# A sixth row buffer for the expert stage, gathers issued five at a time, Pool drains moved, and the last product on two engines

## The chip, the cores and the metric

The kernel runs on one core of one Trainium2 chip. Its engines are called here as the profile calls them: PE (TensorE, matmuls; PEld is its weight load), DVE (VectorE), ACT (ScalarE), Pool (GpSimd) and SP (SyncE, which only issues DMAs). The metric is the device time of one execution in microseconds (us). A row of a profile is stamped in us from the start of the execution.

## The reference, cut to what matters

The program is two transformer blocks over 512 tokens of width 1024, in float32. Of the second block only its end bears on the change: a mixture of 32 experts in 4 groups, two experts per token, and the last norm.

```python
h2 = rmsnorm_2(x, norm2_g[l])
x = x + hier_moe(h2, ...)      # per token: gate * (silu(h @ w_gate[e]) * (h @ w_up[e])) @ w_down[e], two e
return rmsnorm_2(x, norm_f_g)  # y * rsqrt(mean(y * y) + 1e-6) * g
```

An expert has three matrices of 1 MB each (1024x256, 1024x256 and 256x1024).

## The kernel before, in words

Everything ahead of the expert stage (about the first 1050 us) is dense layers and attention; the change leaves it as it is. By the end of it the 512 rows going into the experts lie in DRAM as `x_rows`, and `part_rows`, also 512 rows in DRAM, holds zeros.

The expert stage works in 17 **units** (`UNITS_E`, q = 0 to 16, `LAST_E` = 16). A unit is two halves of 64 rows, each for one expert, so it takes the weights of two experts, 6 MB (unit 8, `EXTRA_AT`, uses one expert for both halves). A small routing program on DVE writes the table `tabi`, a column per unit: which rows to gather (1), where to scatter (0), and for which tokens this is the second and last expert (2), whose rows are finished. Entries for nothing are out of bounds and skipped. What that program finds out late (more rows for an expert than fit, the experts of the later units) it signals as `over_listed` and `over_ready`; the latter comes from `name_late_experts` in unit 1.

Per unit the steps are these; the engines run apart and meet at semaphores:

- **Pool** gathers the rows of the unit from `x_rows` into a row buffer `xe` (L691, `gather`, up to four units ahead, `X_FIRST`), later gathers the partial results from `part_rows` into the same buffer (L699, `gather_parts`, "the parts"), scatters the unit's sum back (L695, `scatter`) and stores the finished rows to `out` (L703, `store_rows`). All are indirect DMAs of Pool's own queue, issued in program order. Parts of unit q+1 may only be gathered once the scatter of unit q has landed (`scattered`). For units 8 and 9 (`MIXED_E`) this stands behind the other steps of the unit before instead of ahead of them.
- **PE** transposes the gathered rows (L2066, `turn_rows_of`), multiplies with the gate and up weights (L2408, `gate_up_part`), transposes the hidden rows (L2066, `turn_hidden`) and multiplies with the down weights (L2425, `down`). For units 1 to 12 (`AHEAD_E`) the first quarter of the gates is done ahead, beside the unit before.
- **DVE** scales the transposed rows (L1759), makes the hidden product (L1766, `hidden`), adds the down result onto the parts (L1776, `y_of`) and, one unit later, multiplies the finished rows by their norm factor and by `gfin`, the final norm vector (L1787, `finish`). It works in program order, so `hidden` of unit q+1 stands behind `y_of(q)` and `finish(q-1)`.
- **ACT** makes the silu (L1159), copies (L1162), and sums squares for the norm (L1170, `squares_of`) in two halves of 512 columns; it ends in a guess of the inverse root that DVE refines.
- **SP** issues all weight loads, each as soon as the buffer is free: six gate/up buffers (`gu`, three units) and eight down buffers (`dn`, four units). For units 3 and 4 (`PIECED_E`) gates and ups are loaded by quarters as PE frees them (L613). SP also loads `gfin` (L602).

The last unit is done by halves of 512 columns: down, `y` (L2004), squares; then DVE's `finish` and Pool's last store. `pool.drain()` stands at q = 13 and 15 (L742), ahead of the wait for `y_made`.

Space sets where the row buffers lie. `xe` has six of 4 KB per partition. Buffers 4 and 5 lie over the scratch tables of the routing program, so before `over_listed` and `over_ready` only four can be filled. The order of use is:

```python
def buffer_of(q):
    return q if q < X_FIRST else (0, 1, 4, 5, 2, 3)[(q - X_FIRST) % X_BUFS]
```

`gfin` lies over the rotation tables (`cos`, `sin`), which are no longer needed by then.

## Time and profile before

| | |
|---|---|
| median of three runs | 1306.07 us (1304.95 to 1306.09) |
| the profiled execution: its own time | 1303.1 us |
| the profiled execution: span from first to last instruction | 1301.1 us |
| mean granted clock of PE | 0.992 of full speed (2.4 GHz) |
| busy share of PE / DVE / ACT / Pool | 96% / 49% / 40% / 44% |
| matmuls L2408 (gate and up), 1088 of them | 128.4 us, 386 ns each |
| matmuls L2425 (down), 256 of them | 61.4 us, 624 ns each |
| DMAs of gates, ups and downs: median time from issue to landing | 15.4, 16.3 and 17.8 us |
| DMA rate in the 34th to 39th of 40 slices | 386, 417, 416, 417, 417 and 417 GB/s, the slices before 331 and 359 |

How to read it: the shares of busy time are means over very different stages. The expert stage is the last fifth, and its limit is to be read from that stretch alone. The span and the profiled time are one execution, 3 us under the median of the runs. A wait in the profile is given as idle time of an engine ahead of an instruction, with what ended it. Pool's busy time counts the issue of a DMA (about 1 us each), not its transfer; "us to landing" is from issue until the last piece has arrived.

### The profile page before, as it was taken

How to read it: one execution, taken by the hardware profiler on the slowest of the kernel's cores; microseconds unless marked ns; L12 is line 12 of the kernel's file. 1: busy time of each engine (PE TensorE's matmuls, PEld its weight loads, DVE VectorE, ACT ScalarE, POOL GpSimd, SP SyncE). 2: the span in 40 equal slices, each digit the busy share in tenths (PEclk: the TensorE clock that was granted, in tenths of full speed). 3: DMA queues.
4: the chain of work that ended last, by engine and by line, in shares of the span. 5: the costliest groups of instructions: out<-in, count | busy, mean ns of one | idle time of the engine just before them, and what ended most of it. 6: DMA issues, size and time to landing. Idle time of an engine off the chain costs nothing.

```text
span 1301.1 us, 18979 instructions
## 1 busy us (share of the span) xinstructions
PE 1255.3 (96%) x6642; PEld 960.5 (74%) x6642; DVE 640.0 (49%) x1248; ACT 522.9 (40%) x884; POOL 568.9 (44%) x715
## 2 busy tenths in 40 slices
PE   7999999999999999999999999999999989998896
PEld 6767777787888888888888788777888865554462
DVE  4868768725542422222225765757243276342443
ACT  5657544435444324133144534145322300543444
POOL 4633323334655655555545664424644212341321
PEclk9999999999999999999999999999999999998899
DMA  6422222112334333333333333322427999999996
GB/s 219 109 65 55 67 58 65 50 49 81 98 96 113 115 97 97 115 97 113 97 98 97 97 96 83 82 49 70 126 81 265 359 331 386 417 417 416 417 417 246
DMA packets 223104, 208.38 MB, mean 160 GB/s; under 512 B 36034, under 2 KB 197556, under 8 KB 218804
## 3 DMA queue, kind: packets, MB, share of 16 engines
q1 hardware_dynamic: 209728, 191.87, 44.7%
q0 software_dynamic: 9504, 13.66, 2.8%
q10 hardware_dynamic: 3796, 1.86, 0.5%
q8 instruction: 45, 0.74, 0.2%
q14 instruction: 31, 0.25, 0.1%
HBM read 209.43 MB, written 20.45 MB: 177 GB/s over the span
## 4 chain that ended last, share of the span: by engine, by line
issue 40%; POOL 31%; PE 19%; DMA 4%; DVE 3%; SPq 2%; POOLq 1%; ACT 0%; DVEq 0%; ACTq 0%
POOL wlo L670 31%; PE bank L2408 4%; PE bank L2036 3%; PE bank L2038 3%; PE bank L2037 3%; PE bank L2425 3%; SPq L543 1%; DMA gu<-in_w_exp_up 1%; DMA xe<-part_rows,tabi 1%; PE side L2066 1%; DMA part_rows<-xe,tabi 1%; DMA xe<-x_rows,tabi 1%; PE side L2038 1%; PE side L2037 1%; PE side L2036 1%
## 5 line engine op out<-in xcount | busy, mean ns | idle before, releaser
L670 POOL TENSOR_TENSOR wlo<-raw,whi 128x256 fp32r<-128x256 f32 x644 | 497.6, 804 | 525.9 <-ACT whi L838 525.7
L2037 PE MATMUL bank<-actB_lo,whi 128*128 128x512 f32 x608 | 236.7, 389 | 0.0
L838 ACT ACTIVATE whi<-raw 128x1024 fp32r<-128x1024 f32 x161 | 169.0, 1051 | 152.6 <-PE bank L2038 125.0
L2036 PE MATMUL bank<-actB_hi,whi 128*128 128x512 f32 x576 | 227.8, 395 | 0.5 <-POOL wlo L670 0.5
L2038 PE MATMUL bank<-actB_hi,wlo 128*128 128x512 f32 x576 | 224.4, 390 | 0.0
L2036 PE MATMUL bank<-actA_hi,whi 128*128 128x512 f32 x400 | 157.0, 392 | 1.7 <-DVE actA_lo L1269 1.6
L2038 PE MATMUL bank<-actA_hi,wlo 128*128 128x512 f32 x400 | 155.7, 389 | 0.0
L2037 PE MATMUL bank<-actA_lo,whi 128*128 128x512 f32 x400 | 155.7, 389 | 0.0
L2408 PE MATMUL bank<-gu,xeT 128*64 128x256 f32 x1088 | 128.4, 386 | 8.5 <-issue 5.9
L2037 PEld LDWEIGHTS bank<-actB_lo,whi 128*128 128x128 f32 x608 | 114.2, 188 | 24.0 <-issue 1.0
L2036 PEld LDWEIGHTS bank<-actB_hi,whi 128*128 128x128 f32 x576 | 108.2, 188 | 25.9 <-issue 2.3
L2038 PEld LDWEIGHTS bank<-actB_hi,wlo 128*128 128x128 f32 x576 | 108.1, 188 | 22.8
L2408 PEld LDWEIGHTS bank<-gu,xeT 128*64 128x64 f32 x1088 | 80.6, 139 | 51.5 <-issue 19.3
L2059 PE MATMUL bank<-actA_hi,whi 128*128 128x512 f32 x216 | 95.0, 440 | 0.0
L2036 PEld LDWEIGHTS bank<-actA_hi,whi 128*128 128x128 f32 x400 | 75.1, 188 | 19.5 <-DVE actA_lo L1269 3.5
L2038 PEld LDWEIGHTS bank<-actA_hi,wlo 128*128 128x128 f32 x400 | 75.1, 188 | 15.8
L2037 PEld LDWEIGHTS bank<-actA_lo,whi 128*128 128x128 f32 x400 | 75.1, 188 | 15.3 <-issue 0.2
L1464 DVE TENSOR_SCALAR relu_u<-bank 128x512 f32<-128x512 f32 x32 | 22.1, 692 | 128.7 <-PE bank L2038 128.7
L2061 PE MATMUL bank<-actA_hi,wlo 128*128 128x512 f32 x216 | 85.0, 393 | 0.0
L2060 PE MATMUL bank<-actA_lo,whi 128*128 128x512 f32 x216 | 84.5, 391 | 0.0
L1478 DVE TENSOR_TENSOR ytmp<-bank,rs 128x512 f32<-128x512 f32 x32 | 22.1, 692 | 95.8 <-PE bank L2038 95.8
L2425 PE MATMUL bank<-dn,hidT 128*64 128x512 f32 x256 | 61.4, 624 | 2.7 <-ACT hidT L1162 2.7
(448 smaller groups left out, 1703.3 us busy)
## 6 DMA issues: line engine op xcount, KB each, us to landing
gu<-in_w_exp_gate SPq DMA_DIRECT2D x64, 512.0 KB, 15.4
gu<-in_w_exp_up SPq DMA_DIRECT2D x64, 512.0 KB, 16.3
dn<-in_w_exp_down SPq DMA_DIRECT2D x30, 1024.0 KB, 17.8
raw<-in_w_in SPq DMA_DIRECT2D x57, 512.0 KB, 3.8
raw<-in_w_up SPq DMA_DIRECT2D x32, 512.0 KB, 3.9
raw<-in_w_down SPq DMA_DIRECT2D x32, 512.0 KB, 3.7
raw<-in_w_out SPq DMA_DIRECT2D x16, 512.0 KB, 3.8
raw<-in_w_in SPq DMA_DIRECT2D x16, 256.0 KB, 3.2
```

Source lines behind the costliest of these rows:

```text
L670: ins = nc.gpsimd.tensor_tensor(wlo[:, slot, at], raw[:, slot, at], whi[:, slot, at].bitcast(F32), ALU.subtract)
L838: a(whi[:, c % RING, :], raw[:, c % RING, :], ACT.Copy).then_inc(hi_made, 1)
L1464: chain(v.tensor_scalar(relu_u[:, m % 2, :], out_bank(up + m)[:, :], 0.0, None, ALU.max), chunk_freed)
L1478: chain(v.tensor_tensor(ytmp[:, :], out_bank(c)[:, :], rs[:, :], ALU.mult), chunk_freed)
L2036: mm(b[:, :], w_hi, hi[:, k, :], start=first, stop=False)
L2037: mm(b[:, :], w_hi, lo[:, k, :], start=False, stop=False)
L2038: ins = mm(b[:, :], w_lo, hi[:, k, :], start=False, stop=last)
L2059: mm(b[:, :], w_hi, actA_hi[:, k, :], start=k == 0, stop=False)
L2060: mm(b[:, :], w_hi, actA_lo[:, k, :], start=False, stop=False)
L2061: ins = mm(b[:, :], w_lo, actA_hi[:, k, :], start=False, stop=k == NK - 1)
L2408: ins = mm(b[ROWS * h:ROWS * (h + 1), g * DE:(g + 1) * DE], xeT[:, j, k, ROWS * h:ROWS * (h + 1)], gu[n % GU_BUFS][:, g, k, :], start=k == ...
L2425: ins = mm(bank[2 + n][ROWS * h:ROWS * (h + 1), :], hidT[:, j, k * P + ROWS * h:k * P + ROWS * (h + 1)], w[:, k, n * L:(n + 1) * L], start ...
```

## The change

- **A row buffer elsewhere.** `xe` shrinks to five buffers, and the sixth, `xe_far`, lies where `gfin` was, over the rotation tables. It is free from the start. `buffer_of` becomes (5, 4, 0, 1, 2, 3) from unit 4 on, so unit 4 uses the new buffer and unit 5 the one over the scratch tables.
- **Gathers.** Five gathers are issued at once instead of four. The gather of unit 5 waits for `over_listed` alone and no longer for the scatter of unit 1; the waits for scatters 0 and 1 and for `over_ready` go.
- **The norm vector in two pieces.** `gfin0` lies over another table (`before`) and is loaded where `gfin` was; `gfin1` lies behind the five buffers, over routing scratch, so SP waits for `over_ready` first, after the quarters of unit 4. DVE waits for both pieces in unit 3. Each product by the norm is two instructions of 512 columns instead of one of 1024.
- **Drains.** The drain at q = 13 goes, that at q = 15 stays; at q = 7 and 8 a drain is put in behind the store, ahead of `scattered(q)` and the parts of units 8 and 9.
- **The last unit.** `finish_last`: DVE multiplies both halves by the norm vector once each half's squares are taken (`last_squared`), then refines the norm (`last_norm_made`), then DVE scales the first half and ACT the second; Pool's last store waits for both.
- The path for overflowing rows gets the same pieces and other semaphore counts; it isn't run with these inputs.

The diff, cut to its core (the lines of `x_in` in place of `xe[:, n, :]` are shown once):

```diff
@@ -42,7 +42,7 @@
 
 def buffer_of(q):
 
-    return q if q < X_FIRST else (0, 1, 4, 5, 2, 3)[(q - X_FIRST) % X_BUFS]
+    return q if q < X_FIRST else (5, 4, 0, 1, 2, 3)[(q - X_FIRST) % X_BUFS]
 
 
 OVER_X = buffer_of(LAST_E + 1)
...
@@ -362,13 +362,13 @@
         dn_at = (*(s_at + n * half_buf for n in range(7)), b_at + 3 * half_buf)
         gu = [place(f"gu{n}", [P, 2, NK, DE], gu_at[n]) for n in range(GU_BUFS)]
         dn = [place(f"dn{n}", [P, 2, D], dn_at[n]) for n in range(D_BUFS)]
-        xe, _ = lay(b_at, ("xe", [P, X_BUFS, D]))
+        xe, gfin_at = lay(b_at, ("xe", [P, X_BUFS - 1, D]))
         hid, row_at, after4, after8, end3 = lay(s_at + 7 * half_buf, ("hid", [P, 2, DE]), ("row_at", [P, 2 * NT]),
                                  ("after4", [P, NG, NG]), ("after8", [P, EPG, EPG]))
...
@@ -377,9 +377,14 @@
         steps64, tabi, over_n, over_at, spare_rows, tab_end = lay(low_at + words([P, 2, NK, P]) + words([P, 2, DE]),
                                        ("steps64", [P, 8]), ("tabi", [P, 3, COLS], I32), ("over_n", [1, 2 * OVER + 1], I32),
                                        ("over_at", [P, 3], I32), ("spare_rows", [P, 1], I32))
-        below = place("below", [1, OVER, NE], b_at + words([P, X_FIRST + 1, D]))
+        below = place("below", [1, OVER, NE], gfin_at)
         slotv = place("slotv", [P, 2, COLS], -(-tab_end // 64) * 64)
-        gfin = place("gfin", [P, D], base + 4 * CONST_COLS["cos"][0])
+        xe_far = place("xe_far", [P, D], base + 4 * CONST_COLS["cos"][0])
+        gfin = (place("gfin0", [P, L], base + 4 * CONST_COLS["before"][0]), place("gfin1", [P, L], gfin_at))
+
+        def x_in(n):
+            return xe[:, n, :] if n < X_BUFS - 1 else xe_far[:, :]
+
         lg, gw, vals, pos, pos_q, over_v, _ = lay(
             base + 4 * CONST_COLS["cos_tok"][0], ("lg", [P, NT, NG + NE]), ("gw", [P, 16, NT]),
             ("vals", [P, 2 * NT, 3]), ("pos", [P, 2 * NT]), ("pos_q", [P, 2 * NT]), ("over_v", [P, 4]))
...
                 sp.wait_ge(S(f"x_stored{n}"), 16 * NK // 2)
-            sp.dma_start(gfin[:, :], A["norm_f_g_2"].partition_broadcast(P)).then_inc(S("small_in"), 16)
+            sp.dma_start(gfin[0][:, :], A["norm_f_g_2"][0:L].partition_broadcast(P)).then_inc(S("small_in"), 16)
             def gate_up_in_quarters(q):
...
@@ -621,6 +626,9 @@
                         down(n)
                 if q in PIECED_E:
                     gate_up_in_quarters(q)
+                    if q == PIECED_E.stop - 1:
+                        sp.wait_ge(S("over_ready"), 1)
+                        sp.dma_start(gfin[1][:, :], A["norm_f_g_2"][L:].partition_broadcast(P)).then_inc(S("small_in"), 16)
                     continue
                 for n in places_of(q):
                     sp.wait_ge(S("gate_up_done"), unit_of(n - GU_BUFS) + 1)
...
             def gather(n, rows, done):
-                pool.indirect_dma_start(xe[:, n, :], None, x_rows, bass.IndirectOffsetOnAxis(ap=rows, axis=0),
+                pool.indirect_dma_start(x_in(n), None, x_rows, bass.IndirectOffsetOnAxis(ap=rows, axis=0),
                                         bounds_check=row_bound, oob_is_err=False).then_inc(done, 16)
 
...
 
-            for q in range(X_FIRST):
-                gather(q, tabi[:, 1, q:q + 1], S(f"gathered{q}"))
+            for q in range(X_FIRST + 1):
+                gather(buffer_of(q), tabi[:, 1, q:q + 1], S(f"gathered{q}"))
...
@@ -738,23 +746,21 @@
                     scattered(q - 1)
                 if FINISH_FROM <= q + 1 < LAST_E and q + 1 not in MIXED_E:
                     parts_of_unit(q + 1)
-                if q in (LAST_E - 3, LAST_E - 1):
+                if q == LAST_E - 1:
                     pool.drain()
                 pool.wait_ge(S("y_made"), q + 1)
                 scatter(buffer_of(q), tabi[:, 0, q:q + 1], S(f"scattered{q % 2}"))
                 n = q + X_FIRST
-                if n < UNITS_E:
-                    if q < 2:
-                        scattered(q)
-                    if q == 2:
+                if X_FIRST < n < UNITS_E:
+                    if q == 1:
                         pool.wait_ge(S("over_listed"), 1)
-                        pool.wait_ge(S("over_ready"), 1)
                     if q - 2 >= FINISH_FROM:
                         pool.wait_ge(S("rows_stored"), 16 * (q - 1 - FINISH_FROM))
                     gather(buffer_of(n), tabi[:, 1, n:n + 1], S(f"gathered{n % X_BUFS}"))
                 if q > FINISH_FROM:
                     store_unit(q - 1)
                 if q + 1 in MIXED_E:
+                    pool.drain()
                     scattered(q)
                     parts_of_unit(q + 1)
             over = over_count(pool)
...
@@ -788,6 +794,7 @@
             scattered(LAST_E - 1)
             for n in range(X_BUFS):
                 pool.wait_ge(S(f"gathered{n}"), 16 * ((LAST_E - n) // X_BUFS + 1))
+            pool.wait_ge(S("last_squared"), 3)
             store_unit(LAST_E)
 
 
...
@@ -1167,7 +1174,8 @@
                 nc.scalar.preload_act_table_set("natural_log_exp_and_others")
                 for n in range(2):
                     act.wait_ge(*((S("y_made"), q + 1) if q < LAST_E else (S("last_y_made"), n + 1)))
-                    chain(a(side[3][:, :], xe[:, buffer_of(q), n * L:(n + 1) * L], ACT.Square, accum_out=gw[:, 10 + n, one_]))
+                    chain(a(side[3][:, :], x_in(buffer_of(q))[:, n * L:(n + 1) * L], ACT.Square, accum_out=gw[:, 10 + n, one_]),
+                          S("last_squared") if q == LAST_E else None)
                     if n == 0:
                         chain(a(gw[:, 3, one_], gw[:, 10, one_], ACT.Identity, scale=1.0 / D, bias=eps_t[:, :]))
                 chain(a(gw[:, 14, one_], gw[:, 11, one_], ACT.Ln, scale=1.0 / D, bias=gw[:, 3, one_]))
...
@@ -1784,8 +1795,22 @@
                 refine(gw[:, 12, one_], gw[:, 13, one_], D, gw[:, 14, one_], gw[:, 15, one_])
                 if q < LAST_E:
                     dve.wait_ge(S(f"scattered{q % 2}"), 16 * (q // 2 + 1))
-                chain(v.scalar_tensor_tensor(xe[:, buffer_of(q), :], xe[:, buffer_of(q), :], gw[:, 13, one_], gfin[:, :],
-                                             ALU.mult, ALU.mult), S("rows_finished"))
+                for n in range(2):
+                    x = x_in(buffer_of(q))[:, n * L:(n + 1) * L]
+                    ins = v.scalar_tensor_tensor(x, x, gw[:, 13, one_], gfin[n][:, :], ALU.mult, ALU.mult)
+                chain(ins, S("rows_finished"))
+
+            def finish_last():
+
+                one_ = slice(LAST_E % NT, LAST_E % NT + 1)
+                first, second = (x_in(buffer_of(LAST_E))[:, n * L:(n + 1) * L] for n in range(2))
+                for n, x in enumerate((first, second)):
+                    dve.wait_ge(S("last_squared"), n + 1)
+                    chain(v.tensor_tensor(x, x, gfin[n][:, :], ALU.mult))
+                dve.wait_ge(S("guess_made"), guesses[0] + 1)
+                chain(v.tensor_tensor(gw[:, 12, one_], gw[:, 10, one_], gw[:, 11, one_], ALU.add))
+                refine(gw[:, 12, one_], gw[:, 13, one_], D, gw[:, 14, one_], gw[:, 15, one_], made=S("last_norm_made"))
+                chain(v.tensor_scalar(first, first, gw[:, 13, one_], None, ALU.mult), S("rows_finished"))
 
             every_expert = const("iota")[:, 0:NE]
             cnt, extra, upto, before = (prod[:, 0, NE * n:NE * (n + 1)] for n in range(4))
...
                     rows_turned(q % 2, q + 3)
                 y_of(q)
-                if q == FINISH_FROM:
-                    dve.wait_ge(S("small_in"), 16 * (N_SMALL + 1))
+                if q == FINISH_FROM + 1:
+                    dve.wait_ge(S("small_in"), 16 * (N_SMALL + 2))
...
             dve.wait_ge(S(f"parts_in{LAST_E % 2}"), 16 * ((LAST_E - FINISH_FROM) // 2 + 1))
             for n in range(2):
-                x = xe[:, buffer_of(LAST_E), n * L:(n + 1) * L]
+                x = x_in(buffer_of(LAST_E))[:, n * L:(n + 1) * L]
                 dve.wait_ge(S("last_down_done"), n + 1)
                 v.scalar_tensor_tensor(x, bank[2 + n][:, :], slotv[:, 1, LAST_E:LAST_E + 1], x,
                                        ALU.mult, ALU.add).then_inc(S("last_y_made"), 1)
-            finish(LAST_E)
+            finish_last()
 
```

How the instructions stand on the engines. **Pool, start of the expert stage**, before (`xe<-x_rows` is a gather of rows, `xe<-part_rows` one of parts, `part_rows<-xe` a scatter):

```order
L691 DMA xe<-x_rows,tabi 128x1024 [waits rows_ready,x_stored1,x_stored0]
L691 DMA xe<-x_rows,tabi 128x1024 x3
L695 DMA part_rows<-xe,tabi 512x1024 [waits y_made,y_zeroed,slots_ready]
L691 DMA xe<-x_rows,tabi 128x1024 [waits scattered0]
L699 DMA xe<-part_rows,tabi 128x1024 [waits xe_used,scattered0]
L695 DMA part_rows<-xe,tabi 512x1024 [waits y_made]
L691 DMA xe<-x_rows,tabi 128x1024 [waits scattered1]
L699 DMA xe<-part_rows,tabi 128x1024 [waits xe_used,scattered1]
L695 DMA part_rows<-xe,tabi 512x1024 [waits y_made]
L691 DMA xe<-x_rows,tabi 128x1024 [waits over_ready,over_listed]
```

and now (`xe_far` is the new buffer):

```order
L699 DMA xe<-x_rows,tabi 128x1024 [waits rows_ready,x_stored1,x_stored0]
L699 DMA xe<-x_rows,tabi 128x1024 x3
L699 DMA xe_far<-x_rows,tabi 128x1024
L703 DMA part_rows<-xe,tabi 512x1024 [waits y_made,y_zeroed,slots_ready]
L707 DMA xe<-part_rows,tabi 128x1024 [waits xe_used,scattered0]
L703 DMA part_rows<-xe,tabi 512x1024 [waits y_made]
L699 DMA xe<-x_rows,tabi 128x1024 [waits over_listed]
L707 DMA xe<-part_rows,tabi 128x1024 [waits xe_used,scattered1]
L703 DMA part_rows<-xe,tabi 512x1024 [waits y_made]
L699 DMA xe<-x_rows,tabi 128x1024
```

The fifth gather stands with the first four, the one behind the first scatter is gone, and the next gather stands behind the second scatter with a wait for `over_listed` where it waited for `scattered1`. Drains are not listed in these rows; the diff shows their place.

**SP, end of the quarters of unit 4** (`gu_140`, `gu_141`) and the down weights of unit 5 (`dn_146`, `dn_147`), before:

```order
L613 DMA gu_140<-in_w_exp_up 128x1024 [waits gate_up_done]
L613 DMA gu_141<-in_w_exp_up 128x1024
L548 DMA dn_146<-in_w_exp_down 128x2048 [waits down_done]
L548 DMA dn_147<-in_w_exp_down 128x2048 [waits down_done]
L543 DMA gu_142<-in_w_exp_gate 128x1024 [waits gate_up_done]
```

and now:

```order
L618 DMA gu_140<-in_w_exp_up 128x1024 [waits gate_up_done]
L618 DMA gu_141<-in_w_exp_up 128x1024
L631 DMA gfin_176<-in_norm_f_g 128x512 [waits over_ready]
L553 DMA dn_146<-in_w_exp_down 128x2048 [waits down_done]
L553 DMA dn_147<-in_w_exp_down 128x2048 [waits down_done]
L548 DMA gu_142<-in_w_exp_gate 128x1024 [waits gate_up_done]
```

The second piece of the norm vector, with its wait, stands ahead of the down weights and all that follows.

**DVE, the end of the program**, from the second half of the last y, before (`gw` are the norm's small values):

```order
L2004 SCALAR_TENSOR_TENSOR xe<-bank,slotv,xe 128x512 [waits last_down_done]
L1783 TENSOR_TENSOR gw<-gw 128x1 [waits guess_made]
L1232 TENSOR_SCALAR gw<-gw 128x1 [waits guess_made,dve_step]
L1233 TENSOR_TENSOR gw<-gw 128x1 [waits dve_step]
L1234 TENSOR_TENSOR gw<-gw 128x1 [waits dve_step]
L1235 SCALAR_TENSOR_TENSOR gw<-gw 128x1 [waits dve_step]
L1787 SCALAR_TENSOR_TENSOR xe<-xe,gw,gfin 128x1024 [waits dve_step]
```

and now:

```order
L2031 SCALAR_TENSOR_TENSOR xe_far<-bank,slotv,xe_far 128x512 [waits last_down_done]
L1809 TENSOR_TENSOR xe_far<-xe_far,gfin_175 128x512 [waits last_squared]
L1809 TENSOR_TENSOR xe_far<-xe_far,gfin_176 128x512 [waits last_squared,dve_step]
L1811 TENSOR_TENSOR gw<-gw 128x1 [waits guess_made,dve_step]
L1243 TENSOR_SCALAR gw<-gw 128x1 [waits guess_made,dve_step]
L1244 TENSOR_TENSOR gw<-gw 128x1 [waits dve_step]
L1245 TENSOR_TENSOR gw<-gw 128x1 [waits dve_step]
L1246 SCALAR_TENSOR_TENSOR gw<-gw 128x1 [waits dve_step]
L1813 TENSOR_SCALAR xe_far<-xe_far,gw 128x512 [waits last_norm_made]
```

The 1024 wide product at the end became two products by the vector ahead of the norm's five small steps and one scaling of 512 columns behind them.

## Rows read from the trace of the kernel before

**Rows 1.** windows, 1096 to 1283 us (columns in its first line)

```profile
core 0: us, PE busy (x) PEld busy (x) DVE busy (x) ACT busy (x) POOL busy (x), PEclk, DMA share, GB/s
...
1096.00:1283.00 187.00, 169.07 (x1204) 95.34 (x1202) 68.17 (x145) 80.58 (x151) 58.39 (x54) 0.95 1.03 416
```

**Rows 2.** chain of waits at the end: start us, us, what

```profile
1264.90 18.86 DMA gu<-in_w_exp_up
...
1295.98 1.29 DVE xe L1787
```

**Rows 3.** timeline of PE: start us, us, what [idle before <-releaser]

```profile
1093.68 1.15 PE L2066 MATMUL side<-con,xe 128*128 128x128 f32 x8 [0.89 <-DMA xe<-x_rows,tabi]
...
1107.39 1.15 PE L2066 MATMUL side<-con,xe 128*128 128x128 f32 x8 [1.55 <-DMA xe<-x_rows,tabi]
...
1144.73 1.08 PE L2408 MATMUL bank<-gu,xeT 128*64 128x256 f32 x8
...
1206.52 0.69 PE L2066 MATMUL side<-con,hid 128*128 128x128 f32 x2 [4.11 <-DVE hid L1766]
...
1273.11 0.44 PE L2066 MATMUL side<-con,hid 128*128 128x128 f32 x2 [1.56 <-DVE hid L1766]
...
1283.80 3.67 PE L2408 MATMUL bank<-gu,xeT 128*64 128x256 f32 x32 [0.81 <-DMA gu<-in_w_exp_up]
```

**Rows 4.** timeline of DVE, the last instruction ahead of over_ready

```profile
1093.50 0.14 DVE L1908 CAST over_n<-prod 1x1 int32<-1x1 f32 x1
```

**Rows 5.** DMA issues near 1073, 1087 and 1125 us, last column us to landing

```profile
dn<-in_w_exp_down SPq DMA_DIRECT2D x2, 1024.0 KB, 6.2
...
dn<-in_w_exp_down SPq DMA_DIRECT2D x2, 1024.0 KB, 11.1
...
gu<-in_w_exp_gate SPq DMA_DIRECT2D x1, 512.0 KB, 19.1
```

**Rows 6.** Pool drains: ns min/median/max, first and last start us

```profile
L742 POOLq DRAIN  x2: 1967/6010/10054, 1247.0 to 1274.4; - x2
...
L257 POOLq DRAIN  x1: 3053/3053/3053, 1297.9 to 1297.9; - x1
```

**Rows 7.** timeline of Pool, the DMAs around the drains

```profile
1167.62 1.03 POOL L703 DMA_INDIRECT out<-xe,tabi  x1 [0.31 <-issue]
1177.13 1.02 POOL L699 DMA_INDIRECT xe<-part_rows,tabi  x1 [8.48 <-DMA part_rows<-xe,tabi]
...
1189.86 1.02 POOL L703 DMA_INDIRECT out<-xe,tabi  x1 [0.31 <-issue]
1194.30 1.02 POOL L699 DMA_INDIRECT xe<-part_rows,tabi  x1 [3.43 <-DMA part_rows<-xe,tabi]
...
1247.20 1.02 POOL L699 DMA_INDIRECT xe<-part_rows,tabi  x1 [3.28 <-DMA part_rows<-xe,tabi]
1257.78 1.02 POOL L695 DMA_INDIRECT part_rows<-xe,tabi  x1 [9.55 <-issue]
...
1298.07 0.98 POOL L703 DMA_INDIRECT out<-xe,tabi  x1 [6.49 <-DVE xe L1787]
```

**Rows 8.** DMA issues near 1167, 1189, 1247 and 1298 us: us to landing

```profile
out<-xe,tabi POOLq DMA_INDIRECT x1, 12.4
...
out<-xe,tabi POOLq DMA_INDIRECT x1, 10.2
...
xe<-part_rows,tabi POOLq DMA_INDIRECT x1, 7.5
...
out<-xe,tabi POOLq DMA_INDIRECT x1, 2.6
```

**Rows 9.** waits, 1045 to 1302 us: us in total, times, longest

```profile
DVE xe L1776 <- DMA xe<-part_rows,tabi: 25.3, 2, 14.4
```

**Rows 10.** instructions on tile xe: duration ns min/median/max

```profile
L1776 DVE SCALAR_TENSOR_TENSOR xe<-bank,slotv,xe x32: 740/748/753, 1075.1 to 1280.2; 128x512 f32<-128x512 f32 x32
L1170 ACT ACTIVATE side<-xe x30: 601/601/603, 1111.7 to 1293.7; 128x512 f32<-128x512 f32 x30
```

69 lines of the change are left out of this document (37 added, 32 removed).

## The prediction, as put on record

> **What bounds the kernel now.** I read four views: the busy time by stretches, the chain of waits at the end, the timelines of PE, SP, DVE and Pool over the expert stage, and the DMA issues of single moments with their time to landing. Up to about 1050 us the change moves nothing, so only the expert stage counts. From 1096 to 1283 us the 16 DMA engines are full: 416 GB/s at a share of 1.03, while PE works 169 of 187 us [rows 1]. So the expert weights arrive at a fixed pace, and their stream ends when its bytes are through. The chain ends accordingly: the last quarter of up weights, issued at 1264.90, lands 18.86 us later, and then come the last matmuls and the norm [rows 2]. But PE is nearly as late. It waits for those weights a mere 0.81 us, and from 1207 us on no other wait of it is longer than the 1.56 us at 1273.11 [rows 3]. Two limits lie on each other: the end moves with whichever gets later, and an early PE gains nothing. What can be delayed without harm is 0.81 us on PE and nothing on the stream.
>
> **Part 1: the second piece of the final norm vector (SP).** SP now waits for over_ready behind the quarters of unit 4, ahead of the down weights of unit 5. DVE's last instruction ahead of that signal ends at 1093.64 [rows 4]; SP issued those down weights at 1087.66, as the DMA issues of that moment show [rows 5]. So it stands some 6 us, and all of the stream's later issues are queued behind it. What hides part of this is the queue: the last quarters land near 1093 us. A pair of down weights issued into a nearly empty queue, at 1073.0, took 6.2 us in the median; the pair of 1087.66 took 11.1 behind the backlog and landed about 1087.85 + 11.1 = 1098.95 [rows 5]. New: the norm piece goes out at 1093.7, the pair at about 1094.2, and lands at 1094.2 + 6.2 + 0.6 (256 KB at 416 GB/s) = 1101.0. The stream shifts by **+2.1 us**. Bounds: 0 (the queue still had bytes, and the traffic of Pool fills the hole) and +3.5 (all of the time between 1093.0 and the first bytes of an issue at 1094, plus the piece itself).
>
> **Part 2: five gathers at once (Pool).** Row buffer 5 now lies where the rotation tables were, so unit 4 needs no buffer freed by unit 0, and unit 5 goes after scatter 1 is issued, not after it has landed. The two stalls of PE for gathered rows, 0.89 and 1.55 us [rows 3], go: PE is 2.44 us earlier from unit 4 on. What is late next are the gate weights of unit 7: issued at 1125.0, landed 19.1 us later at 1144.1 [rows 5], and PE used them at 1144.73 [rows 3], 0.6 us after. With the stream 2.1 us late, PE stands there until 1146.2. So ahead of unit 8 PE is 2.1 - 0.6 = **1.5 us later** than before, and the 2.44 us are spent. The fifth gather itself, about a microsecond of Pool, falls into an idle stretch: 0.
>
> **Part 3: the drains (Pool).** This is the large term. The trace records three drains. They end at 1247.0 + 10.05 = 1257.0, at 1274.4 + 1.97 = 1276.4 and at 1297.9 + 3.05 = 1300.9 [rows 6]. The parts issued at 1247.20 landed 7.5 us later, at 1254.7, and the scatter behind the first drain went out only at 1257.78, 9.55 us idle [rows 7, 8]. An empty drain would have taken nothing. I read a drain on Pool as a wait for every DMA it has in flight. The one removed (unit 13) delayed a scatter that nobody waited for, since PE's longest wait after 1207 us is that 1.56 us for `hidden` of unit 15; worth 0. The one kept (unit 15) stays. The two new ones stand at units 7 and 8, behind the gather and the store and ahead of the wait for the scatter. The program waited there for the scatter alone; now it waits for the store issued 2.65 us behind it as well.
> Unit 7: the store issued at 1167.62 took 12.4 us and landed at 1180.0; the parts of unit 8 went out at 1177.13 [rows 7, 8]. New: 1180.0 + 1.5 (part 2) + 0.25 (the nearer of the two ends to a landing seen, the last drain) + 0.3 (issue) = 1182.1, that is +4.9. Their landing released y of unit 8 after DVE had stood idle for them, the longer (14.4 us) of its two waits for parts, 25.3 us together [rows 9]: fully on the path. So scatter, gather and store of unit 8 are 4.9 later too.
> Unit 8: the store issued at 1189.86 took 10.2 us: 1200.1 + 4.9 = 1205.0, with 0.55 again 1205.5; the parts of unit 9 went out at 1194.30 [rows 7, 8]: **+11.2**. DVE stood idle for them too, the other 10.9 us [rows 9], and behind y of unit 9 on DVE stand the product of unit 8 and `hidden` of unit 10, for which PE waited 4.11 us at 1206.52 [rows 3]. Nothing cushions that; PE is 11.2 us late from there to the end. That unit's down weights can't help, since PE's wait is for DVE.
> What each drain ends behind its last landing is between 0.25 us (last drain: the store of 1298.07 took 2.6, so 1300.7, and the drain ended at 1300.9 [rows 6 to 8]) and 2.3 us (first: 1254.7, ended 1257.0); I take 0.25, as there a store was last in flight, as here. The other end adds 2 x 2.05 = 4.1 us.
>
> The Trainium skill (DMA: Bandwidth & Descriptors, Anatomy of one DMA) gives a Pool DMA about 2.0 us plus its bytes at 436 GB/s; by that estimate a store would land 2.65 us after the scatter ahead of it, each drain would cost 2.65 + 0.55 = 3.2, and the sum below would be +6.8 instead of +10.1. The rows here say 10.2 and 12.4 us for one store, so the trace does not agree, and the sum goes by the rows.
>
> **Part 4: products and the tail.** The product by the norm vector, once 1024 wide, is now two of 512. Nearest row: 0.75 us each [rows 10], 1.50 against the 1.29 of the chain [rows 2]; I take +0.15 as two of one line overlap (0.0 to 0.2), on the path once, ahead of `hidden` of unit 10. In the last unit DVE multiplies both halves by the vector while ScalarE finds the norm. The second half has to wait for the second square and ends about 0.2 us behind the guess; then after the refinement the two engines scale a half each, ScalarE in 0.60 us [rows 10], instead of 1.29 on DVE alone. Net: 0.2 + 0.05 + 0.6 - 1.29 = **-0.45 us**, between 0 and -0.8. The new `last_squared` wait of Pool stands with the wait it had.
>
> **Sum.** PE path: 11.2 + 0.15 - 0.81 (its slack) - 0.45 = **+10.1 us**. The stream's own end (+2.1 - 0.45) lies below that and is hidden. SP's issues for units 14 to 16 wait for a PE that is 11 us late, but the last loads took some 18.9 us to land because they queued [rows 2], where 6.2 is what an empty queue takes [rows 5]: the queue has nearly 13 us to give, and the stream ends before PE asks for it: 0. The profiled execution took 1303.1 us with a span of 1301.1; the median of the runs is 1306.07. The sum is put on the median: **1316.0 us**. What can be told from no change is 0.2%, or 2.6 us: 1303.5 to 1308.7.
>
> **The rivals.**
> (a) *A new drain costs nothing*: it ends when the scatter has landed, as the program waited there anyway. For it: the drain at 1274.4 took only 2 us, and none of the records shows what it looks at. Against it: the 9.55 us gap. Then the stream is the bound, +2.1 - 0.45 = +1.65: **1307.7**, 1305.5 to 1309.5 with the bounds of part 1.
> (b) *Faster*: the pace of the stream is set by SP's issues, and these by PE's releases, so the two vanished gather stalls come through. Place: gathers 4 and 5, from 1093 us on. Price: -2.44 - 0.45 = -2.9: **1303.2**. It decides if the queue doesn't run dry at over_ready and the drains are free as in (a). Against it: a DMA share of 1.03 for 187 us.
> (c) *Drains end late*, 2.3 us behind each landing like the first one: +14.2, **1320.3**; I count it with the forecast.
> (d) *The extra buffer is no help*: gather 5 lands after PE wants it, 1.55 us stay. PE stands for the gates of unit 7 anyway, so the end is that of the forecast; only the trace would tell.
>
> **How the numbers follow.** Forecast with (c): 0.75; its own range is from 8.0 (stream shift 0, so PE is 0.6 us early at unit 7 and not 1.5 late) to 10.1 + 4.1 + 1.4 = 15.6 us, 1314 to 1321.7. (a) 0.19, (b) 0.03, slower for another reason 0.03. The range reaches down into (a) at 1307.5 and up to 1321.5; that leaves out about 0.2. Faster: (b) and a sliver of (a), 0.04. Same: most of (a), 0.16. Slower: 0.80.
>
> **What would show it.** Right: drain records at units 7 and 8 of 10 us or more, the parts of unit 9 issued some 11 us later, a PE wait near 15 us ahead of the transposes of unit 10 where 4.11 stood, no PE wait for the last up weights, a DMA share under 1 after 1215 us. SP's pair of down weights near 1094 us with a hole in the stream before it; no PE wait for x_rows; a PE wait of some 4 us for the gates of unit 7. Wrong: short drains with parts of unit 9 within 3 us of their old place relative to PE, or a last PE wait for up weights still there.

## The result, and the profile after

| | before | after |
|---|---|---|
| median | 1305.51 us (1303.0 to 1306.09, 4 runs) | 1321.53 us (1319.77 to 1325.15, 4 runs) |
| ratio to before | 1 | 1.0130, 95% interval 1.0104 to 1.0156 |
| the profiled execution: time, span | 1303.1, 1301.1 us | 1319.77, 1317.7 us |
| mean granted clock of PE | 0.992 | 0.984 |

The changed kernel is slower by 16 us. I had forecast 10 (1316.0, from 1307.5 to 1321.5; 1306.07 + 10.1 is in fact 1316.2): the direction was right, the amount too small, and the result lies just above the range.

Where the time comes in is read from PE's starts at fixed places of the program:

| PE starts | before | after | later by | forecast |
|---|---|---|---|---|
| first gates of unit 0 | 1057.70 | 1058.66 | 0.96 | 0 |
| first gates of unit 7 | 1144.73 | 1149.10 | 4.37 | 1.5 |
| first gates of unit 9 | 1174.91 | 1180.61 | 5.70 | 1.5 |
| transposes of `hidden` of unit 10 | 1206.52 | 1221.59 | 15.07 | 11.2 |
| down products of the last unit | 1289.15 | 1305.86 | 16.71 | 10.5 |
| end of the span | 1301.1 | 1317.7 | 16.6 | 10.1 |

Between units 9 and 10 stand the two new drains: 9.4 us, where I had 9.7. All other stages gave more than I had. PE's timeline of the changed kernel, at the places of [rows 3]:

```profile
1058.66 7.13 PE L2435 MATMUL bank<-gu,xeT 128*64 128x256 f32 x64 [0.71 <-DVE xeT L1770]
...
1149.10 1.98 PE L2435 MATMUL bank<-gu,xeT 128*64 128x256 f32 x8 [5.02 <-DMA gu<-in_w_exp_gate]
...
1180.61 1.98 PE L2435 MATMUL bank<-gu,xeT 128*64 128x256 f32 x8 [3.11 <-issue]
...
1221.59 0.69 PE L2093 MATMUL side<-con,hid 128*128 128x128 f32 x2 [7.97 <-DVE hid L1777]
...
1249.34 0.44 PE L2093 MATMUL side<-con,hid 128*128 128x128 f32 x2 [1.33 <-DVE hid L1777]
1250.46 5.35 PE L2452 MATMUL bank<-dn,hidT 128*64 128x512 f32 x16 [0.68 <-ACT hidT L1169]
...
1297.09 7.11 PE L2435 MATMUL bank<-gu,xeT 128*64 128x256 f32 x64
```

The waits for gathered rows (0.89 and 1.55 us in [rows 3]) are gone, and so is the wait for the last up weights: the 64 matmuls at 1297.09 run in one piece. In their place stands 5.02 us for the gates of unit 7 and 7.97 for `hidden` of unit 10. The first eight gate matmuls behind the 5.02 us take 1.98 us, where they take 1.08 at full clock: the granted clock is at its lower level there (1.2 GHz; it is 0.50 from 1150 to 1152 us). Unit 12's down products take 5.35 instead of 3.65 for the same reason.

SP's side, with the stretches of the DMA engines (us, then busy time of each engine, PEclk, DMA share, GB/s), of the changed kernel:

```profile
1094.64 0.33 SPq L631 DMA_DIRECT2D gfin<-in_norm_f_g  x1
1095.01 1.05 SPq L553 DMA_DIRECT2D dn<-in_w_exp_down  x2
```

```profile
1088.00:1092.00 4.00, 4.00 (x38) 2.54 (x36) 3.23 (x7) 0.00 (x0) 1.38 (x2) 1.00 1.03 413
1092.00:1096.00 4.00, 4.00 (x36) 2.52 (x31) 3.58 (x15) 0.74 (x1) 1.41 (x2) 1.00 0.78 282
1096.00:1100.00 4.00, 4.00 (x24) 1.67 (x24) 0.45 (x1) 0.38 (x1) 0.42 (x1) 1.00 0.89 276
1100.00:1104.00 4.00, 4.00 (x38) 2.49 (x36) 1.68 (x4) 0.00 (x0) 1.28 (x2) 1.00 1.00 404
```

and the last three of these stretches of the kernel before:

```profile
1092.00:1096.00 4.00, 3.11 (x26) 1.91 (x22) 3.41 (x11) 0.70 (x1) 0.00 (x0) 1.00 1.04 428
1096.00:1100.00 4.00, 4.00 (x24) 1.66 (x24) 0.00 (x0) 0.38 (x1) 0.03 (x1) 1.00 0.99 411
1100.00:1104.00 4.00, 4.00 (x38) 2.50 (x36) 1.74 (x4) 0.00 (x0) 3.08 (x4) 1.00 1.03 420
```

The hole that the prediction spoke of is there, and it is larger: in twelve microseconds (428 - 282 + 411 - 276 + 420 - 404) x 4 = 1.2 MB less are moved, 2.9 us at 416 GB/s. What is moved holds the piece as well, 0.25 MB or 0.6 us, so by this count the weights fall back by 3.5 us.

The drains (ns min/median/max, first and last start), and Pool's DMAs around them, of the changed kernel:

```profile
L763 POOLq DRAIN  x2: 10698/11452/12207, 1175.0 to 1198.2; - x2
```

```profile
1173.47 1.01 POOL L703 DMA_INDIRECT part_rows<-xe,tabi  x1 [7.70 <-DVE xe L1787]
...
1187.98 1.02 POOL L707 DMA_INDIRECT xe<-part_rows,tabi  x1 [10.80 <-issue]
1196.66 1.01 POOL L703 DMA_INDIRECT part_rows<-xe,tabi  x1 [7.66 <-DVE xe L1787]
...
1209.66 1.02 POOL L707 DMA_INDIRECT xe<-part_rows,tabi  x1 [9.29 <-issue]
```

The records last 12.2 and 10.7 us. They begin ahead of the store's own issue (1175.0 and 1198.2, the stores at 1176.17 and 1199.35), so they are a little longer than what Pool stands for: 10.8 and 9.3 us idle ahead of the parts. The parts of unit 9 go out 13.0 us behind the scatter of unit 8; before it was 1194.30 [rows 7] less 1187.21, the scatter's issue there, or 7.1.

### The profile page after: what moved, and what is told of

It is laid out like the page before. It is cut to its first block, busy times and chain, and to the rows that moved or that the text cites. A ratio compares the mean times of both kernels' runs of the same rounds, so it can differ in the third digit from the quotient of the medians.

```text
span 1317.7 us, 19000 instructions
## 1 busy us (share of the span) xinstructions
PE 1264.5 (96%) x6642; PEld 967.5 (73%) x6642; DVE 637.2 (48%) x1264; ACT 523.4 (40%) x885; POOL 566.3 (43%) x715
## 4 chain that ended last, share of the span: by engine, by line
issue 40%; POOL 31%; PE 20%; DMA 3%; DVE 3%; SPq 2%; POOLq 1%; ACT 1%; another core or an unknown queue 0%; DVEq 0%; ACTq 0%
POOL wlo L678 31%; PE bank L2435 6%; PE bank L2452 3%; PE bank L2063 3%; PE bank L2065 3%; PE bank L2064 3%; DMA gu<-in_w_exp_gate 2%; SPq L548 1%; DMA xe<-part_rows,tabi 1%; PE side L2093 1%; SPq L553 1%; PE side L2063 1%; PE side L2065 1%; PE side L2064 1%; PE side L2351 0%
## 5 line engine op out<-in xcount | busy, mean ns | idle before, releaser
L2452 PE MATMUL bank<-dn,hidT 128*64 128x512 f32 x256 | 64.5, 650 | 4.8 <-ACT hidT L1169 4.1
```

Source lines behind the costliest of these rows:

```text
L2452: ins = mm(bank[2 + n][ROWS * h:ROWS * (h + 1), :], hidT[:, j, k * P + ROWS * h:k * P + ROWS * (h + 1)], w[:, k, n * L:(n + 1) * L], start ...
```

## The experiments

Eleven kernels ran. All times are medians of several runs, beside the kernel before on the same chip; 0.2% is 2.6 us. "Drains" are the two new ones, "piece" is SP's load of the second half of the norm vector with its wait for `over_ready`.

### Drains and piece, alone and together

No new drains (`e1`):

```diff
                 if q + 1 in MIXED_E:
-                    pool.drain()
                     scattered(q)
```

> The changed kernel without its two new Pool drains (units 7 and 8); the old one at unit 15 stays. Theory (the drains wait for all of Pool's DMAs in flight and cost PE 9.4 us of the 16, the rest is a weight stream some 4.5 us late): the end falls back to where the late stream sets it, 1308 to 1312 us, and PE waits for the last up weights again, or for hidden(10) near 6 us instead of 7.97. Rival A (the drains end with the scatter and cost little, the 16 us come from the late stream and what it triggers): 1317 to 1321. Rival B (drains are everything, the late stream is hidden): 1304 to 1306.

1310.59 us against 1304.29, ratio 1.0045 (1.0032 to 1.0058). The changed kernel stands at 1.0130, so in its surroundings the two drains are worth 0.85% or 11 us, more than the 9.4 of the table. PE's wait for `hidden` of unit 10 is 3.96 us, as before the change (4.11). The theory holds, with about 6 us left for everything else.

The kernel before with the two drains (`e2`, the same line added):

> The kernel before with nothing but two drains more, at units 7 and 8, ahead of the wait for the scatter. Theory: parts(8) about 5 us later, parts(9) about 10 to 11, PE 9 to 10 us late from unit 10 on, less 0.8 of slack: +8.5 to +10, and up to +12 if the later stall lowers the granted clock behind it as in the changed kernel: 1314 to 1317.5. Rival A: within 1 us of before. It also tells whether the first gate matmuls of unit 0 start at 1057.7 (then the 0.96 us of the changed kernel come from its fifth gather or norm piece) or at 1058.7.

1309.73 us against 1304.29, ratio 1.0055 (1.0034 to 1.0076), so some 7 us (4.4 to 9.9): in the median less than the 8.5 to 10 expected, but far from rival A. In the profiled execution PE is 8.9 us late at `hidden` of unit 10 (1215.40), which is what was expected; at the last down products it is 5.8 us late. On the way it has used the 0.81 us of slack, and the down products of unit 15 take 3.66 us in it where they take 5.31 in the kernel before (the clock again); these two are 2.5 of the 3.1 us. The first gates of unit 0 start at 1057.86: the late start doesn't come from the drains.

The piece moved behind the first half of unit 5's weights (`e3`, in the changed kernel):

```diff
                     gate_up_in_quarters(q)
-                    if q == PIECED_E.stop - 1:
-                        sp.wait_ge(S("over_ready"), 1)
-                        sp.dma_start(gfin[1][:, :], ...)
                     continue
                 for n in places_of(q):
                     sp.wait_ge(S("gate_up_done"), unit_of(n - GU_BUFS) + 1)
                     gate_up(n)
+                    if n == 2 * PIECED_E.stop:
+                        sp.wait_ge(S("over_ready"), 1)
+                        sp.dma_start(gfin[1][:, :], ...)
```

> The changed kernel with the second piece of the norm vector, and the wait for over_ready, moved behind the gate and up weights of the first half of unit 5, where the signal has come already: SP never stands for it. Theory: the hole in the stream at 1094 closes, the down weights of unit 5 go out near 1088 again, gates of unit 7 are wanted before or just when they land (PE wait there under 1.5 us instead of 5.0), and the end comes 3.5 to 6 us earlier than in the changed kernel: 1315 to 1318. Rival (the drains alone set the end, PE has room ahead of them): no change, 1321. Rival 2 (the stream is late from its start at 1058, not from this wait): 0 to 2 us earlier.

1318.95 us, ratio 1.0112 (1.0097 to 1.0127), some 2 us less than the changed kernel; the intervals overlap, and 3.5 to 6 us had been expected. PE's wait for the gates of unit 7 goes from 5.02 to 2.30 us, not under the 1.5 expected.

Both (`e4`):

> The changed kernel with both: piece of the norm vector later and no new drains. What is left of the change is the sixth row buffer, five gathers at once, no drain at unit 13, and the last product on two engines. Theory: the stream is the bound as before and only the tail counts (0.3 to 0.8 us less), minus what the start at unit 0 costs (0 to 1 us more): 1304 to 1306, no difference from before or a little faster. Rival (the pace of the stream is set by PE's releases, so the gather stalls come through): 1302 to 1303.5.

1306.29 us, ratio 1.0016 (1.0007 to 1.0026). In shares of the time: 1.30% with both, 0.45% without the drains, 1.12% without the early piece, 0.16% without either. The piece is worth 0.29% (3.7 us) where no drain stands behind it and 0.18% where one does. The rival that expected a gain from the vanished gather stalls falls. What is left of the change still costs 2 us, just outside the 1304 to 1306 expected, which neither drains nor piece explain.

### What a drain waits for

In units 7 and 8 the order is changed so that the drain stands right behind the scatter, and gather and store come after the parts (`e6`, in the changed kernel, the piece early):

```diff
                 scatter(buffer_of(q), ...)
+                if q + 1 in MIXED_E:
+                    pool.drain()
+                    scattered(q)
+                    parts_of_unit(q + 1)
                 n = q + X_FIRST
...
                     store_unit(q - 1)
-                if q + 1 in MIXED_E:
-                    pool.drain()
-                    scattered(q)
-                    parts_of_unit(q + 1)
```

> The changed kernel with its drains, but in units 7 and 8 the order is scatter, drain, wait for the scatter, parts, and only then gather and store, so that the scatter is the last of Pool's DMAs in flight at the drain. Theory (a drain ends with the last DMA in flight): drains of about 8 us, parts(9) 8 to 8.5 us behind scatter(8) (13.0 in the changed kernel, 7.8 without drains), and the time is that of the kernel without new drains or a little less: 1307 to 1311. Rival (a drain behind an indirect DMA costs several us whatever is in flight): drains over 10 us, 1317 to 1321.

1308.17 us against 1304.43, ratio 1.0030 (1.0018 to 1.0042). Both drains are still executed, and 1.0 of the 1.3% is gone, some 13 us. The edit changes two things at once, since the parts now also go out ahead of the gather and the store. Against `e1`, without drains and in the old order (1.0045), `e6` is even 0.15% or 2 us faster, so that order brings something of its own: without drains it is 0.13% (`e8` below against `e5`), within what the intervals can tell. Its two drains, and the scatter of unit 8 with the parts of unit 9:

```profile
L754 POOLq DRAIN  x2: 8226/8452/8679, 1175.5 to 1193.8; - x2
```

```profile
1194.06 0.99 POOL L703 DMA_INDIRECT part_rows<-xe,tabi  x1 [5.43 <-DVE xe L1787]
1202.86 1.04 POOL L707 DMA_INDIRECT xe<-part_rows,tabi  x1 [7.80 <-issue]
```

8.8 us from scatter to parts instead of 13.0. A drain lasts until the last DMA issued ahead of it has landed, so its price is set by its place in the queue, as the theory says. By the trace's last completion record of each DMA, the first scatter of `e6` landed at 1182.86, and the drain ended at 1184.21. In `e2` (both drains) and `e11` the last store landed at 1179.6, 1203.4 and 1207.0, and the drain ended at 1181.0, 1203.6 and 1208.6; in the changed kernel it is 1185.8 and 1208.7, with ends at 1187.2 and 1208.9. That is 0.2 to 1.6 us behind; the drain of unit 13 in the kernel before (2.3 us, in the prediction) is the longest.

One drain alone, at unit 8 (`e11`, in the changed kernel):

> The changed kernel with the new drain at unit 8 alone, none at unit 7. Theory (drains wait for the store behind the scatter, each costs about 5 us on the path, 9.4 together): parts(8) as without drains, 7.7 us behind scatter(7); parts(9) 12.5 to 13 us behind scatter(8); 4.5 to 5.5 us less than the changed kernel: 1315 to 1317. Rival (the first drain's delay makes the second one shorter, so that one alone costs nearly all): 1319 to 1321.

1314.54 us against 1304.00, ratio 1.0078 (1.0063 to 1.0093), 0.5% less than with both. Its profiled execution doesn't go with that: it took 1316.4 us, the drain lasted 12.8 us, and PE waited 11.52 us for `hidden` of unit 10, which it reached at 1221.14, only 0.45 us ahead of the changed kernel. Part of that is not the drain's: PE came to unit 9 at 1182.36, 1.75 us behind the changed kernel. From the gates of unit 9 to `hidden` of unit 10 it is 31.6 us in `e1`, 38.8 in `e11` and 41.0 in the changed kernel, so in the traces the drain of unit 8 alone costs 7.1 us and that of unit 7 another 2.2. The reason can be seen: in `e11` the scatter of unit 8 had landed at 1201.86 and the parts went out 7.5 us later (1209.40), where it is 5.5 us in the changed kernel (1204.12 and 1209.66) and 0.3 before the change. So the rival is right in kind, one drain makes the other cheaper; medians say some 6.8 us for unit 7 and 4.3 for unit 8, and the exact split stays open.

### Where the stream is lost

The kernel before with nothing but SP's wait (`e7`):

```diff
                     gate_up_in_quarters(q)
+                    if q == PIECED_E.stop - 1:
+                        sp.wait_ge(S("over_ready"), 1)
                     continue
```

> The kernel before with nothing but SP's wait for over_ready ahead of the down weights of unit 5; no second piece. Theory (the wait empties the queue; the piece is only 0.6 us of it): down weights issued at 1093.9 instead of 1087.66, the stream 2.5 to 3.5 us late at 1100 to 1150 us and, being the bound at the end, 2 to 3.5 us later end: 1306.5 to 1308. Rival 1 (my forecast: 2.1 us less the piece, 1.5): 1305.5 to 1306. Rival 2 (the small broadcast piece is what stops the stream): stream not late by over 1 us, 1304 to 1305.

1307.10 us against 1304.43, ratio 1.0019 (1.0010 to 1.0028), 2.7 us. The wait alone does it. Its stretches:

```profile
1092.00:1096.00 4.00, 3.75 (x32) 2.26 (x28) 2.90 (x10) 1.11 (x2) 1.02 (x1) 1.00 0.75 233
1096.00:1100.00 4.00, 4.00 (x26) 1.55 (x24) 0.26 (x1) 0.00 (x0) 1.00 (x1) 1.00 0.98 406
1100.00:1104.00 4.00, 4.00 (x40) 2.70 (x38) 1.42 (x4) 0.00 (x0) 2.03 (x2) 1.00 1.02 348
```

(428 - 233 + 411 - 406 + 420 - 348) x 4 = 1.1 MB, or 2.6 us, are lost without any second piece. Not all of it is an empty queue: from 1100 to 1104 us the share is 1.02, so the engines were busy and moved less. For the weights even this count is too low, as it takes in Pool's DMAs, of which two went out 5 us earlier here. SP's queue alone moved 6.92 MB between 1086 and 1104 us in the kernel before and 5.37 in `e7`, 3.7 us at 416 GB/s. At unit 7 PE gets its gates at 1148.29, 3.56 us later than before.

What the piece adds is not to be seen. From the first gates of unit 0 to those of unit 7 PE takes 87.0 us before, 90.9 in `e7` (the wait, no piece), and 90.4, 90.7, 90.2 and 91.3 in the changed kernel, `e1`, `e6` and `e11` (wait and piece). With the piece later it takes 87.5 and 87.8 (`e3`, `e4`). So the wait is worth 3 to 4 us on PE there, with the piece or without.

### The late start

The first gate matmul of unit 0 stands 7.36 us behind the first gather in the kernel before and 7.40 in `e2`, but 8.3 to 8.5 in the changed kernel, `e1`, `e3` and `e4`. These have the five gathers in a row. In `e5` the fifth goes out after the slot table is ready (from `e4`):

```diff
-            for q in range(X_FIRST + 1):
+            for q in range(X_FIRST):
                 gather(buffer_of(q), ...)
             pool.wait_ge(S("slots_ready"), 1)
+            gather(buffer_of(X_FIRST), ...)
```

> As the run with the later norm piece and without new drains (1306.3 us against 1304.3 before), but the fifth gather goes out only once the slot table is ready (about 1059 us instead of 1055.6). In the four runs with five gathers in a row the first gate matmul of unit 0 starts 8.3 to 8.5 us behind the first gather, in the two with four gathers 7.4. Theory (the fifth gather behind the first four holds up unit 0): the distance falls to 7.4, the weight stream starts 1 us earlier and the end comes about 1 us earlier: 1304.5 to 1305.5. Rival (it is the layout of buffers or code, not the gather): 8.4 and 1306.3 stay.

1305.79 us against 1304.43, ratio 1.0010 (1.0001 to 1.0019). The distance is 1056.92 - 1049.58 = 7.34 us, as before the change, and 7.32 and 7.68 in `e8` and `e9` below, which hold the fifth gather back too. `e10`, which also does, spoils the series: 8.82 us, since the first gather itself landed late there (PE waited 1.22 us for it). With five in a row six kernels gave 8.08 to 8.46. So the fifth gather is the likely cause of 1 us, not a proven one. Whether the end gains it is not shown: the medians say -0.5 us against `e4`, or 0.06% in the ratios, less than the intervals can tell.

### A long wait and the clock

In `e5` PE still reached unit 9 2.6 us late (1177.50 against 1174.91), though it had its gates of unit 7 at 1144.43, 0.3 us early. Three kernels more, none with new drains, all with the late piece and the late fifth gather. `e8`: the parts of units 8 and 9 go ahead of gather and store, as in `e6`:

> As the run with the fifth gather later (piece later, no new drains), and in units 7 and 8 the parts of the next unit go ahead of the gather and the store. Theory: the parts land 1 to 3 us sooner behind their issue, since 0.5 MB less stands ahead of them; DVE waits less for them, PE's wait for hidden(10) (4.47 us) shrinks by 2 to 4, and the end comes as early as the weight stream lets it: 1302.5 to 1304.5. Rival (the parts' issue waits for the landed scatter, and nothing else counts; the stream is the bound anyway): no change from the run beside it.

1304.06 us against 1304.43, ratio 0.9997 (0.9988 to 1.0006). As expected the wait ahead of `hidden` of unit 10 is gone, but PE stands 2.93 us for gathered rows at 1206.55 instead, since that gather now goes out behind the parts. PE in and behind unit 7's wait, of `e8`:

```profile
1144.92 1.98 PE L2435 MATMUL bank<-gu,xeT 128*64 128x256 f32 x8 [2.22 <-DMA gu<-in_w_exp_gate]
```

```profile
1145.00:1153.00 8.00, 8.00 (x32) 3.24 (x34) 0.01 (x1) 5.18 (x10) 1.02 (x1) 0.60 1.03 415
```

The same stretch of the kernel before has a clock of 1.00 and 58 matmuls instead of 32. There PE had stood 0.89 and 1.55 us, in two places; here the same slack is one wait of 2.22 us, and a clock at half follows for most of the stretch. The scatter of unit 6 goes out 10.7 us behind the gates of unit 7 (1155.61 - 1144.92), where it was 7.6. `e9` turns `hidden` ahead of those gates, `e10` fills the wait with products that nobody reads:

```diff
+                if q == EXTRA_AT - 2:
+                    turn_hidden(q % 2, q + 1)
                 first_gates_of(q + 1, 0)
-                turn_hidden(q % 2, q + 1)
+                if q != EXTRA_AT - 2:
+                    turn_hidden(q % 2, q + 1)
```

> As the run with the parts first (1304.1 us), and at the end of unit 6 PE turns the hidden rows ahead of the first gates of unit 7 instead of behind them. There PE stood 2.22 us in one piece for those gates, and the granted clock then went to half for 6.8 us, so that unit 8's share of the work started 3 us later relative to the gates than before. Theory (one long stall costs its clock as well; cut in two shorter ones it doesn't, as the two stalls of 0.89 and 1.55 us before the change didn't): no wait over 1.3 us at unit 7, the first gate matmuls there take 1.08 us and not 1.98, the scatter of unit 6 goes out 2 to 3.5 us earlier against those gates, PE is 2 to 3 us earlier at unit 9, and the end comes 0.5 to 1.5 us earlier, where the weight stream ends it: 1302.5 to 1303.6. Rival (the half clock has another cause, such as the sum of the work around it): the same clock drop near 1145 to 1151, 1304.

```diff
+                if q == EXTRA_AT - 2:
+                    pe.wait_ge(S("xe_t_made"), 2 * q + 3)
+                    keep_busy(bank[1 - q % 2], 9)
                 first_gates_of(q + 1, 0)
```

> As the run with the parts first, with nine idle products of ones (about 2.1 us of PE work that nobody reads) where PE stood for the gates of unit 7. Theory: those gates still start near 1144.9, but at full clock (1.08 us, not 1.98), and no clock drop stands between 1144 and 1151; unit 9 about 2 to 3 us earlier than in the run with the parts first; the end 1302.5 to 1303.6. Rival (the drop doesn't come from PE's idle time): drop as before, 1304 or later.

`e9`: 1303.65 us against 1304.00, ratio 1.0005 (0.9996 to 1.0014); `e10`: 1303.75 us, 1.0000 (0.9991 to 1.0009). The clock, `e10` first, then `e9`:

```profile
1145.00:1153.00 8.00, 6.16 (x32) 2.75 (x32) 0.00 (x0) 4.00 (x10) 1.02 (x1) 0.79 1.03 412
```

```profile
1145.00:1153.00 8.00, 7.48 (x38) 3.29 (x40) 0.36 (x1) 3.56 (x9) 1.02 (x1) 0.79 1.02 413
```

My theory expected no drop; there is one, half as long (0.79 instead of 0.60). Neither had removed the wait: PE stood 1.84 us in `e10`, where the gates came later (1147.19) than the filler lasted, and 2.20 in `e9`. From gates to scatter it is 9.3 and 8.8 us, 1.4 and 1.9 us of the 3 won.

That these edits won it is not shown, because two earlier kernels have the same short drop with the wait left as it was. `e3` and `e4`, behind waits of 2.30 and 2.67 us (PE's row, then the stretch):

```profile
1146.95 1.08 PE L2435 MATMUL bank<-gu,xeT 128*64 128x256 f32 x8 [2.30 <-DMA gu<-in_w_exp_gate]
1147.00:1155.00 8.00, 8.00 (x40) 3.44 (x42) 0.42 (x2) 5.18 (x10) 1.02 (x1) 0.79 1.03 414
```

```profile
1146.34 1.08 PE L2434 MATMUL bank<-gu,xeT 128*64 128x256 f32 x8 [2.67 <-DMA gu<-in_w_exp_gate]
1146.00:1154.00 8.00, 7.66 (x38) 3.33 (x40) 0.15 (x2) 5.19 (x10) 1.02 (x1) 0.79 1.03 416
```

Their scatters go out 9.3 and 9.2 us behind the gates, as in `e10`. In all eleven kernels in which PE stood for these gates in one piece, for 1.84 to 6.08 us, the clock fell behind the wait, but by how much doesn't go with its length: the mean over eight microseconds is 0.79 behind waits of 1.84, 2.20, 2.30, 2.67 and 5.02 us, and 0.57 to 0.60 behind 2.22, 2.34, 4.85, 4.95, 5.16 and 6.08. The end didn't move by what an interval can tell. `e9`'s last rows fit that:

```profile
1283.80 3.67 PE L2435 MATMUL bank<-gu,xeT 128*64 128x256 f32 x32 [1.37 <-DMA gu<-in_w_exp_up]
```

PE waits 1.37 us for the last up weights, where it had waited 0.81 [rows 3]. The stream is the bound there again. No version here is faster than the kernel before: `e8`, `e9` and `e10`, with the sixth buffer and the shared last product, equal it.

## Why the prediction was right or wrong

**Part 1, the norm piece: the mechanism right, the size wrong.** This is the step that failed first. The sum had +2.1 us for the stream, 0.6 of it the piece, and so +1.5 on PE at unit 7. The runs show 3.4 us there in the changed kernel, beside 1.0 of late start, and 3.6 in `e7`, which has the wait and no piece. With the 0.6 us by which PE had been behind the gates that is some 4 us of stream, over the upper bound of 3.5 that I had set. I took the hole as the stretch from the landing of the last quarters (1093) to the first bytes of a new issue (1094), and let the landing of the down weights stand for the stream. That landing I had nearly right for the new kernel (1101.0; in `e7` the last one lands at 1101.34), but in the kernel before it was not at 1098.95 but at 1100.26: the 11.1 us are the median over a pair of which the later one is what counts. And it says little of the stream. In `e7` the down weights are 1.1 us late, yet the first gates of unit 5 land at about 1104.7 instead of 1100.61. The rate doesn't drop for one microsecond, it is near half for four (233 GB/s from 1092 to 1096, at a share of 0.75, where it was 428 at 1.04). The share alone would make it 1.1 us; why the engines also moved fewer bytes while busy stays open.

**The late start: not in the prediction.** I had priced the fifth gather at 0, a microsecond of Pool in an idle stretch. In the six kernels with five in a row PE and DVE use the first rows 0.7 to 1.1 us later. I had looked at Pool's idle time and not at who waits meanwhile. The term was put at nothing and came to 1.0 us.

**Part 2, the gathers: right in what it said, incomplete.** The stalls went, and the time went to the gates of unit 7, as forecast. But I took idle time as exchangeable. Behind one longer wait there stands the lower clock level, a term that I had at nothing: the scatter of unit 6 goes out 9.1 us behind the gates of unit 7 instead of 7.6, and behind it the weights of the spare expert, for which unit 9 waits. PE loses 1.3 us more between units 7 and 9 (4.37 to 5.70). No run has the wait without the drop, so that the clock is all of it is argued.

**Part 3, the drains: the mechanism and the sum right, the split not.** Records of 12.2 and 10.7 us (I had said 10 or more); a drain waits for everything of Pool's in flight, which `e6` shows by moving it; no cushion between DVE and PE; 9.4 us on PE where I had 9.7. Behind the gates of unit 9 the parts of unit 8 are 5.2 us late where I had 3.4, those of unit 9 another 4.5 where I had 6.3; that the two errors cancel is luck. The first drain ended 1.4 us behind the landing of its store, where I had 0.25; and the store of unit 8 landed 4.6 us behind its scatter, where it is 6.0 in the kernel before. The end of a drain is 0.2 to 1.6 us behind the landing, all but within my two ends (0.25 and 2.3). The Trainium skill (DMA: Bandwidth & Descriptors, Anatomy of one DMA) gives, as an estimate from its 2.0 us plus bytes at 436 GB/s, a store that lands 2.65 us behind the scatter, and a whole of +6.8. This trace doesn't agree: in `e11` the scatter of unit 8 landed at 1201.86 and the store, issued at 1196.98, at 1207.04, which is 5.2 us behind the scatter and 10.1 us behind its own issue. The rows of this case were the better price.

**Part 4.** Products: the two of 512 take 1.41 to 1.43 us together (I said 1.44). Tail: from the last down products to the end 11.84 us instead of 11.95, -0.11 where I had -0.45. Its end chain, after:

```profile
1311.23 0.70 DVE xe_far L1809
...
1311.96 0.17 DVE gw L1811
...
1312.98 0.73 ACT xe_far L1223
```

The refinement starts 6.10 us behind the last down products instead of 5.87, the 0.2 that I had. From there to Pool's store it is 2.64 instead of 3.05 us. But ScalarE takes 0.72, not 0.60, and the store goes out 0.9 us behind it, not 0.81 as behind DVE.

**Behind the drains.** From unit 10 to the last down products I had -0.7 (0.81 of slack against 0.15 for the products); it was +1.6. The missing 2.3 us are the clock (0.85 in the stretch from 1206 to 1240 us against 0.90, and the row of 5.35 us above) and the 1.33 us wait that follows. `e2` shows the same in the other direction. This term varies from kernel to kernel and I had left it out.

**Signs.** Of the eight, five were seen as given: the drain records, no wait for the last up weights, the late down pair behind a hole, no wait for gathered rows, and (5.02 us for some 4) the wait at unit 7. The parts of unit 9 were 15.4 us later, not 11. The wait ahead of the transposes of unit 10 is 7.97 us, not 15, since PE came there late itself, with 3.29 us of waiting ahead of unit 9's `hidden`. And the DMA share did not fall under 1 at 1215: it is 1.02 from 1206 to 1240 and 1.03 from 1240 to 1283, and the rate breaks off only in the stretch from 1288 to 1292 (201 GB/s). The weights queued ahead carried the stream over PE's long wait. **Rivals.** (a), drains free, is out by `e1` and `e2`; (b), faster, by `e4`; (c), drains that end late, by the drains' own ends. (d) is out, since the gather waits are gone.

The sum, as measured: start 1.0, unit 7 3.4, clock up to unit 9 1.3, drains 9.4, clock and waits behind them 2.4 (with 0.8 of slack spent), tail -0.1: 16.6 us. That is 6.5 over my forecast: 4.2 in the first three (5.7 where I had 1.5), 2.3 in the fifth (1.6 with the slack, where I had -0.7) and 0.3 in the tail; the drains are 0.3 under it. That the result lies so near the top of the range is no merit of the range: its top was made of drains that end late (4.1 us), which they didn't, and 1.4 us of stream.

**Open.** In `e1`, `e3`, `e4`, `e5`, `e6`, `e8` and the changed kernel, PE's signals come some 2 us late near 1165 us, and ACT and DVE stand for them. It isn't there in the kernel before, nor in the other five. It is hidden, since PE waits for the spare expert behind it, and no run was spent on it. Why a fifth gather delays the first rows wasn't tried either, nor what decides whether the clock is low for most or for half of the eight microseconds behind a wait. The drain of unit 13 was never put back by itself, nor the last product put back on one engine; the 0.1 us of the tail is all that the traces show of the latter.

## What to carry to other kernels

Put a Pool drain right behind the transfer that it is for, ahead of all others: with the same two instructions there, and the parts moved up with them, the kernel was 13 us faster. A wait on a queue that issues a saturated stream is priced by all that stands behind it on that queue, not by the moment at which the transfer engines run dry. And where short waits of PE are gathered into one longer wait, look at the granted clock behind it before counting them as the same time. A drop that changes with an edit is only the edit's when kernels without it don't show the same range.
